# Four products of the filter instead of two sums, added by PE in the transform back, in a stage of attention and hyena

## The chip, the core and the metric

The kernel runs on one core of a Trainium2 chip. The metric is the time of one execution on the device in microseconds (us), lower is better. The engines are PE (TensorE, matmul; its weight loads have a row of their own, PEld), DVE (VectorE), ACT (ScalarE), POOL (GpSimd) and SP (SyncE, which here issues most DMA transfers). Each works through its own queue in order, and they meet only at semaphores. PE writes to PSUM, in banks of 512 fp32 columns.

## What is computed

The reference is a backbone of two layers over 1024 latent tokens and 256 context tokens. Each layer projects its input for three groups of heads (a state space scan, differential attention, and a Hyena convolution of order 2), joins their outputs and projects them back. The change lies in the long convolution:

```python
def _fft_long_conv(u, kf, bias):
    """u (B,L,C), kf (L+1,C) -> two-sided long conv over the whole sequence + bias * u."""
    L = u.shape[1]
    uf = jnp.fft.rfft(u.astype(F32), n=2 * L, axis=1)
    y = jnp.fft.irfft(uf * kf, n=2 * L, axis=1)[:, :L]
    return (y + bias.astype(F32) * u.astype(F32)).astype(u.dtype)

def _hyena(proj, conv_w, conv_b, filt, bias):
    L = proj.shape[1]
    v, x1, x2 = jnp.split(_centred_dwconv(proj, conv_w, conv_b), 3, axis=-1)
    kf = _hyena_kernels_fft(L, filt)
    z = x1 * _fft_long_conv(v, kf[:, 0], bias[0])
    return x2 * _fft_long_conv(z, kf[:, 1], bias[1])
```

`uf * kf` is a product of complex numbers: with X the spectrum of the input and K that of the filter, the real part is Xr Kr - Xi Ki and the imaginary part Xi Kr + Xr Ki.

## The kernel before

Every layer runs stages one after the other, with a barrier between them: normalisation, projections, then `attention_hyena_stage` (L1235), the scan, for the first layer the convolution of the context, and the output projection. `attention_hyena_stage` puts two jobs that have nothing to do with each other into one loop of ticks (`for i in range(NI)`), written once for each engine.

The first job is attention. Its units are (head, tile of 128 queries): 4 x 10 in layer 0 and 4 x 8 in layer 1. In layer 0 the first two tiles of a head are context (I call them short: 256 keys), all others have 1280 keys. A unit passes through several ticks. In tick i PE makes its scores in two halves m = 0 and 1 (L1402, L1403), DVE takes the maximum of each (L1586), ACT the exponential (L1517). A tick later DVE mixes the two halves (L1598). Two ticks later PE turns the mix in up to three batches (L1418), ACT copies each (L1524), and PE multiplies with the values (L1434). After that ACT norms, DVE scales (L1604), PE turns (L1423) and DVE gates (L1611).

The second job is the convolution of 1024 latent tokens, 512 channels in four chunks of 128 and two orders: 8 phases of 4 steps, 32 steps, in ticks 3 to 34. In tick i it is step n = i - 3, and s = n mod 4 is its part of the phase. A step has two of the phase's eight blocks of frequencies:

- PE, `forward` (L1448): 8 matmuls of 128x128 in fp32 (L1460, L1461) from R with the matrices fwd into the PSUM bank pH.
- DVE, `products` (L1613): pH times the spectrum of the filter (K, kn), into R. pt is its scratch tile.
- PE, `backward` (L1464): 8 matmuls (L1475) of R with the matrices inv, into pH again. In order 0 the matrices are the loaded side, in order 1 the data are.
- ACT, `copy_back` (L1539, in the next tick): pH to R (L1542).

Around them DVE has the butterflies: `backs` in the first two ticks of a phase for the phase before, `forth` in the other two for the phase after (`Steps`, L1055 to L1068). In ticks 1 to 13 PE also turns the rows of the convolution's input (`turn_rows`, L1445).

The order within a tick is written out by hand. PE: turn 0, scores 0, forward, turn 1, scores 1, last turn, values, rows, backward. DVE: maximum 0, scale, mix, products, maximum 1, gate, butterflies. ACT: copy back, copy of turn 0, norm, copy of turn 1, exponential 0, last copy, exponential 1. The last 256 columns of scores 1 share a bank with scores 0 and wait for exponential 0. SP loads K two steps ahead into one of two buffers, when the products of the step that used it are done (`y_ready`).

Of the kernel before, what the change touches and what calls it, by code (L numbers as in the profile page):

```python
# [14 lines left out]
ALU = mybir.AluOpType  # L15
# [3 lines left out]
P = 128  # L19
# [141 lines left out]
def sb(nc, ctx, name, shape, dtype=F32):  # L161
    return ctx.enter_context(nc.sbuf_tensor(name, list(shape), dtype))
# [1067 lines left out]
def matrix_block(k, i):  # L1230

    return i if k == 0 else 4 + 3 * (k - 1) + (0, 1, 1, 2)[i]


def attention_hyena_stage(nc, tag, layer, first_tile, ident, lam_vecs, qk_d, v_d, gate_d, hp_d, kf_d, fwd_d, inv_d, o_d):  # L1235
# [29 lines left out]
    with stage(nc, tag + "lam_in", tag + "s00_in", tag + "s01_in", tag + "s10_in", tag + "s11_in", tag + "v0_in", tag + "v1_in",  # L1265
# [1 line left out]
               tag + "turned_copied", tag + "pv_done", tag + "squared", tag + "log_done", tag + "rms_ready", tag + "scaled", tag + "o_turned",  # L1267
               tag + "gated", tag + "stored0", tag + "stored1",
               *(tag + "u%d_in" % c for c in range(4)), *(tag + "x%d_in" % c for c in range(4)), *(tag + "k%d_in" % c for c in range(2)), tag + "kn_in",
               tag + "mats_in", tag + "rows_turned", tag + "rows_copied", tag + "dft_step", tag + "r_ready", tag + "x_mm", tag + "prod_step", tag + "y_ready",  # L1270
               tag + "q_mm", tag + "q_copied", tag + "z_step", tag + "out_ready", tag + "hy_stored") as (ctx, sems):
        (lam_in, s00_in, s01_in, s10_in, s11_in, v0_in, v1_in, lam_step, lam_exp, scored, maxed, exped, mix_step, mixed, turned, turned_copied,
         pv_done, squared, log_done, rms_ready, scaled, o_turned, gated, stored0, stored1) = sems[:25]
        u_in, x_in, k_in = sems[25:29], sems[29:33], sems[33:35]
        (kn_in, mats_in, rows_turned, rows_copied, dft_step, r_ready, x_mm, prod_step, y_ready, q_mm, q_copied, z_step, out_ready, hy_stored) = sems[35:]
        stored = (stored0, stored1)
        score_in = ((s00_in, s01_in), (s10_in, s11_in))
        value_in = (v0_in, v1_in)
# [40 lines left out]
        with nc.Block() as block:  # L1319
            @block.sync  # L1320
            def _(sp):
# [20 lines left out]
                def load_spectra(n):  # L1342
                    p, s = divmod(n, 4)
                    c, o = phases[p]
                    if n >= 2:
                        sp.wait_ge(y_ready, n - 1)
                    sp.dma_start(K[:, n % 2], kf_d[o][:, 4 * s:4 * s + 4, P * c:P * (c + 1)]).then_inc(k_in[n % 2], 16)
                    if s == 0:
                        sp.dma_start(kn[:], kf_d[o][:, 2 * J, P * c:P * (c + 1)]).then_inc(kn_in, 16)
# [6 lines left out]
                for n in range(2):  # L1356
                    load_spectra(n)
# [31 lines left out]
            def _(pe):  # L1389
# [177 lines left out]
            def _(dve):  # L1567
# [45 lines left out]
                def products(n):  # L1613

                    p, s = divmod(n, 4)
                    f = phases[p][0] % 2
                    xs = pH[:].rearrange("p (k a n) -> p k a n", k=2, a=2)
                    kr, ki = (K[:, n % 2, i:4:2].unsqueeze(2).to_broadcast([P, 2, 2, P]) for i in range(2))
                    y = R[:, f, 2 * s:2 * s + 2]
                    dve.wait_ge(k_in[n % 2], 16 * (n // 2 + 1))  # L1620
                    dve.wait_ge(x_mm, n + 1)
                    if n:
                        dve.wait_ge(y_ready, n)
                    if s == 0:
                        dve.wait_ge(kn_in, 16 * (p + 1))
                        dve.tensor_tensor(y[:, 1], xs[:, 1], kr[:, 1], ALU.mult).then_inc(prod_step, 1)
                        dve.tensor_tensor(y[:, 0, 0], xs[:, 0, 0], K[:, n % 2, 0], ALU.mult).then_inc(prod_step, 1)
                        dve.tensor_tensor(y[:, 0, 1], xs[:, 0, 1], kn[:], ALU.mult).then_inc(prod_step, 1)
                    else:
                        dve.tensor_tensor(y, xs, kr, ALU.mult).then_inc(prod_step, 3)  # L1630
                    dve.tensor_tensor(pt[:], xs, ki, ALU.mult).then_inc(prod_step, 1)
                    dve.wait_ge(prod_step, 5 * n + 4)
                    dve.tensor_tensor(y[:, :, 0], y[:, :, 0], pt[:, :, 1], ALU.subtract).then_inc(prod_step, 1)
                    dve.tensor_tensor(y[:, :, 1], y[:, :, 1], pt[:, :, 0], ALU.add).then_inc(y_ready, 1)

                def backs(p, first, last):
                    c, o = phases[p]
# [826 lines left out]
```

## Time and profile before

| | us |
|---|---|
| median of 3 runs | 4172.46 (4168.78 to 4177.13) |
| profiled execution, its own time | 4166.99 |
| its span, first to last instruction | 4164.9 |
| this stage in layer 0, first tick's maximum to the last gate | 1143.6 to 1615.9 |
| this stage in layer 1, first maximum to the last store | 3250.6 to 3683.0 |
| busy in the whole span: PE, PEld, DVE, ACT, POOL | 3522.2, 2889.8, 2521.2, 1081.6, 699.4 |
| mean granted clock of TensorE, share of full speed | 0.928 |

A tick begins where DVE starts its first maximum (L1586, half 0). In layer 1 tick 3 begins at 3284.44, tick 5 at 3307.30, tick 14 at 3421.02 and tick 31 at 3634.49. In layer 0 tick 3 begins at 1174.74, tick 5 at 1197.42, tick 10 at 1260.50, tick 14 at 1307.10, tick 30 at 1502.75 and tick 35 at 1557.07.

### The profile page before, as it was taken

How to read it: one execution, taken by the hardware profiler on the slowest of the kernel's cores; microseconds unless marked ns; L12 is line 12 of the kernel's file. 1: busy time of each engine (PE TensorE's matmuls, PEld its weight loads, DVE VectorE, ACT ScalarE, POOL GpSimd, SP SyncE). 2: the span in 40 equal slices, each digit the busy share in tenths (PEclk: the TensorE clock that was granted, in tenths of full speed). 3: DMA queues.
4: the chain of work that ended last, by engine and by line, in shares of the span. 5: the costliest groups of instructions: out<-in, count | busy, mean ns of one | idle time of the engine just before them, and what ended most of it. 6: DMA issues, size and time to landing. Idle time of an engine off the chain costs nothing. (4 is left out here: it accounts for less than half of the span.)

```text
span 4164.9 us, 51062 instructions
## 1 busy us (share of the span) xinstructions
PE 3522.2 (85%) x19424; PEld 2889.8 (69%) x19424; DVE 2521.2 (61%) x5084; ACT 1081.6 (26%) x1861; POOL 699.4 (17%) x444
## 2 busy tenths in 40 slices
PE   5789999999778875996996788999999688859888
PEld 1677888888667774775782566788888577737577
DVE  3125677754279996765553324667773699967544
ACT  2212222222144443332110311222211344423310
POOL 0132333322100001210000122433343000012000
PEclk8899999999888997998998799999999799989999
DMA  4154223232253312334325145223231633123432
GB/s 174 55 142 144 94 85 97 81 101 74 72 162 97 89 35 74 122 98 150 118 81 187 36 115 163 88 81 97 81 100 62 188 84 84 40 100 105 134 115 71
DMA packets 414110, 424.53 MB, mean 102 GB/s; under 512 B 56908, under 2 KB 350540, under 8 KB 412710
## 3 DMA queue, kind: packets, MB, share of 16 engines
q1 hardware_dynamic: 368844, 319.55, 26.5%
q10 hardware_dynamic: 45024, 101.73, 6.9%
q8 instruction: 155, 2.54, 0.3%
q14 instruction: 87, 0.71, 0.1%
HBM read 288.28 MB, written 124.53 MB: 99 GB/s over the span
## 5 line engine op out<-in xcount | busy, mean ns | idle before, releaser
L665 PE MATMUL l_p_acc<-l_u_hi,l_p_w_hi 128*128 128x512 f32 (+1 forms) x2240 | 612.4, 376 | 49.5 <-POOL l_p_w_lo L580 37.0
L665 PE MATMUL l_p_acc<-l_u_hi,l_p_w_lo 128*128 128x512 f32 (+1 forms) x2240 | 593.5, 367 | 0.0
L665 PE MATMUL l_p_acc<-l_u_lo,l_p_w_hi 128*128 128x512 f32 (+1 forms) x2240 | 592.2, 367 | 0.0
L665 PEld LDWEIGHTS l_p_acc<-l_u_hi,l_p_w_hi 128*128 128x128 f32 x2240 | 390.4, 190 | 127.9 <-POOL l_p_w_lo L580 37.5
L665 PEld LDWEIGHTS l_p_acc<-l_u_hi,l_p_w_lo 128*128 128x128 f32 x2240 | 386.0, 189 | 72.4
L665 PEld LDWEIGHTS l_p_acc<-l_u_lo,l_p_w_hi 128*128 128x128 f32 x2240 | 385.8, 189 | 72.3
L578 POOL TENSOR_TENSOR l_p_w_hi<-l_p_wt,l_p_zero 128x1024 fp32r<-128x1024 f32 x104 | 207.7, 1997 | 983.2 <-PE l_p_acc L665 816.2
L1945 POOL TENSOR_TENSOR l_sd_xend<-l_sd_tok,l_sd_mine 128x512 f32<-128x512 f32 x80 | 85.6, 1072 | 1283.0 <-ACT l_sd_tok L1900 1282.2
L1402 PE MATMUL l_at_pS<-l_at_k_hi,l_at_q 128*128 128x512 f32 (+1 forms) x400 | 167.1, 418 | 147.2 <-ACT l_at_prob L1517 113.9
L580 POOL TENSOR_TENSOR l_p_w_lo<-l_p_wt,l_p_w_hi 128x1024 fp32r<-128x1024 f32 x104 | 271.0, 2606 | 8.2
L1586 DVE TENSOR_REDUCE l_at_nmax<-l_at_pS 128x1 f32<-128x1280 f32 (+1 forms) x144 | 197.1, 1369 | 81.7 <-PE l_at_pS L1403 78.7
L1517 ACT ACTIVATE l_at_prob<-l_at_pS,l_at_nmax 128x1280 f32<-128x1280 f32 (+1 forms) x144 | 177.4, 1232 | 249.5 <-DVE l_at_nmax L1586 249.5
L1402 PEld LDWEIGHTS l_at_pS<-l_at_k_hi,l_at_q 128*128 128x128 f32 x400 | 79.6, 199 | 186.3 <-ACT l_at_prob L1517 142.7
L876 DVE TENSOR_SCALAR l_p_cv<-l_p_stg,l_p_taps 128x1281 f32<-128x1281 f32 (+1 forms) x56 | 85.0, 1517 | 192.6 <-ACT l_p_stg L729 192.2
L822 DVE TENSOR_TENSOR l_p_R<-l_p_sw,l_p_rs 128x512 f32<-128x512 f32 x72 | 49.6, 689 | 228.7 <-PE l_p_sw L644 228.7
L1434 PE MATMUL l_at_pO<-l_at_v,l_at_mixT 128*128 128x128 f32 x1312 | 180.5, 299 | 7.6 <-ACT l_at_mixT L1524 4.5
L1434 PEld LDWEIGHTS l_at_pO<-l_at_v,l_at_mixT 128*128 128x128 f32 x1312 | 174.4, 215 | 10.1 <-issue 6.5
L878 DVE SCALAR_TENSOR_TENSOR l_p_cv<-l_p_stg,l_p_taps,l_p_cv 128x1281 f32<-128x1281 f32 (+1 forms) x56 | 150.8, 2692 | 2.0
L1524 ACT ACTIVATE l_at_mixT<-l_at_pT 128x512 f32<-128x512 f32 (+1 forms) x200 | 104.0, 520 | 181.3 <-PE l_at_pT L1418 181.3
L295 PE MATMUL l_n_pm<-l_n_wa,l_n_cond 128*2 128x512 f32 x192 | 88.0, 616 | 68.5 <-DMA l_n_wa<-w_ada 68.5
L1403 PE MATMUL l_at_pS<-l_at_k_lo,l_at_q 128*128 128x512 f32 (+1 forms) x400 | 144.0, 367 | 0.0
L643 PE MATMUL l_p_sw<-l_p_R,l_p_late 128*128 128x128 f32 x528 | 107.4, 286 | 34.0 <-DVEq L815 34.0
(324 smaller groups left out, 7051.2 us busy)
## 6 DMA issues: line engine op xcount, KB each, us to landing
l_p_wt<-w_in SPq DMA_DIRECT2D x104, 512.0 KB, 3.9
l_n_wa<-w_ada SPq DMA_DIRECT2D x12, 2048.0 KB, 8.2
xbc_d<-l_p_fin ACTq DMA_DIRECT2D x32, 640.0 KB, 2.9
kf_d<-l_p_R SPq DMA_DIRECT2D x72, 256.0 KB, 3.6
l_o_oT<-o_d SPq DMA_DIRECT2D x18, 1024.0 KB, 6.7
l_at_K<-kf_d SPq DMA_DIRECT2D x64, 256.0 KB, 2.9
l_o_rows<-w_out SPq DMA_DIRECT2D x32, 512.0 KB, 4.6
qk_d<-l_p_late ACTq DMA_DIRECT2D x12, 1280.0 KB, 4.8
```

Of the source, the lines that this page charges most:

```text
L295: mm = pe.matmul(pm[0:2, (j % 2) * BANK:(j % 2 + 1) * BANK], cond[:, k], wa[:, j % 2, k], start=(k == 0), stop=(k == KD - 1))
L578: pool.tensor_tensor(w_hi[:, m % 2], wt[:, m % 2], zero[:].unsqueeze(2).to_broadcast([P, KD, P]), ALU.add).then_inc(w_rounded, 1)
L580: pool.tensor_tensor(w_lo[:, m % 2], wt[:, m % 2], w_hi[:, m % 2], ALU.subtract).then_inc(w_split, 1)
L643: pe.matmul(out, mats[:, 4 * k + 2 * e], R[:, k, 0, cols], start=True, stop=False)
L665: mm = pe.matmul(acc[:, a:a + w], (w_hi, w_lo)[wp][:, m % 2, k], (u_hi, u_lo)[up][:, k, t0 + c:t0 + c + w], start=(k == n == 0), stop=(k = ...
L878: dve.scalar_tensor_tensor(cv[:, lo:], stg[:, lo:T + 1], taps[:, 0, tile:tile + 1], cv[:, lo:], ALU.mult, ALU.add).then_inc(conv_step, 1)
L1402: pe.matmul(out, q_s[:, s, m, q * P:(q + 1) * P], k_hi[:, s, m, c:c + w], start=True, stop=False)
L1403: mm = pe.matmul(out, q_s[:, s, m, q * P:(q + 1) * P], k_lo[:, s, m, c:c + w], start=False, stop=True)
L1434: mm = pe.matmul(pO[:, 0:P], mixT[:, kt], v_s[:, h % 2, kt], start=(kt == 0), stop=(kt == keys(q) // P - 1))
L1517: act.activation(prob[:, (2 * n + m) % 3, 0:keys(q)], pS[:, m * T:m * T + keys(q)], ACT.Exp, bias=nmax[:, n % 2, m:m + 1], accum_out=sums[ ...
L1524: act.activation(mixT[:, 4 * b:4 * b + w // P].rearrange("p a b -> p (a b)"), pT[:, 0:w], ACT.Copy).then_inc(turned_copied, 1)
L1586: dve.tensor_reduce(nmax[:, n % 2, m:m + 1], pS[:, m * T:m * T + keys(q)], AX.X, ALU.max, negate=True).then_inc(maxed, 1)
```

## The change

`products` no longer adds. It leaves four real products: Xr Kr and Xi Kr in R as before, and in pt, whose two halves are now ordered by the part that they belong to, -Xi Ki (made with `scalar_tensor_tensor` and the constant -1) and Xr Ki. `backward` multiplies both R and pt with the same inverse matrix and lets PSUM add: 4 matmuls in an accumulation group in place of 2, so 16 in a step in place of 8. The two additions of 256 columns on DVE and its wait for its own products (`prod_step`) go, and so does its wait for the step before. `y_ready` now counts 5 in a step, and PE and SP wait for five times the number.

```diff
@@ load_spectra (SP)
-                        sp.wait_ge(y_ready, n - 1)
+                        sp.wait_ge(y_ready, 5 * (n - 1))
@@ backward (PE)
-                    pe.wait_ge(y_ready, n + 1)
+                    pe.wait_ge(y_ready, 5 * (n + 1))
                     for k in (2 * s, 2 * s + 1):
                         for part in range(2):
                             out = pH[:, (2 * (k % 2) + part) * P:(2 * (k % 2) + part + 1) * P]
                             for i in range(2):
                                 m = inv[:, matrix_block(k, 2 * part + i)]
-                                left, right = (m, R[:, f, k, i]) if o == 0 else (R[:, f, k, i], m)
-                                mm = pe.matmul(out, left, right, start=(i == 0), stop=(i == 1))
+                                for j, product in enumerate((R[:, f, k, i], pt[:, i, k % 2])):
+                                    left, right = (m, product) if o == 0 else (product, m)
+                                    mm = pe.matmul(out, left, right, start=(i == j == 0), stop=(i == j == 1))
@@ products (DVE)
-                    kr, ki = (K[:, n % 2, i:4:2].unsqueeze(2).to_broadcast([P, 2, 2, P]) for i in range(2))
+                    kr, ki = (K[:, n % 2, i:4:2] for i in range(2))
                     y = R[:, f, 2 * s:2 * s + 2]
                     dve.wait_ge(k_in[n % 2], 16 * (n // 2 + 1))
                     dve.wait_ge(x_mm, n + 1)
-                    if n:
-                        dve.wait_ge(y_ready, n)
                     if s == 0:
...
                     else:
-                        dve.tensor_tensor(y, xs, kr, ALU.mult).then_inc(prod_step, 3)
-                    dve.tensor_tensor(pt[:], xs, ki, ALU.mult).then_inc(prod_step, 1)
-                    dve.wait_ge(prod_step, 5 * n + 4)
-                    dve.tensor_tensor(y[:, :, 0], y[:, :, 0], pt[:, :, 1], ALU.subtract).then_inc(prod_step, 1)
-                    dve.tensor_tensor(y[:, :, 1], y[:, :, 1], pt[:, :, 0], ALU.add).then_inc(y_ready, 1)
+                        dve.tensor_tensor(y, xs, kr.unsqueeze(2).to_broadcast([P, 2, 2, P]), ALU.mult).then_inc(y_ready, 3)
+                    dve.tensor_tensor(pt[:, 1], xs[:, :, 0], ki, ALU.mult).then_inc(y_ready, 1)
+                    dve.scalar_tensor_tensor(pt[:, 0], xs[:, :, 1], -1.0, ki, ALU.mult, ALU.mult).then_inc(y_ready, 1)
```

Lines of this stage behind the backward loop stand one higher after the change (the maximum is L1587, the matmul of the transform back L1476).

DVE, the products of one step in layer 1 (part 2 of a phase), with what each instruction waits for. Before:

```order
L1598 SCALAR_TENSOR_TENSOR l_at_mix<-l_at_prob,l_at_back 128x1280 [waits l0_at_turned,l0_at_mix_step]
L1630 TENSOR_TENSOR l_at_R<-l_at_pH,l_at_K 128x512 [waits l0_at_x_mm,l0_at_y_ready,l0_at_k1_in]
L1631 TENSOR_TENSOR l_at_pt<-l_at_pH,l_at_K 128x512
L1633 TENSOR_TENSOR l_at_R<-l_at_R,l_at_pt 128x2x128 [waits l0_at_prod_step]
L1634 TENSOR_TENSOR l_at_R<-l_at_R,l_at_pt 128x2x128
L1586 TENSOR_REDUCE l_at_nmax<-l_at_pS 128x1 [waits l0_at_scored]
```

The same place after:

```order
L1599 SCALAR_TENSOR_TENSOR l_at_mix<-l_at_prob,l_at_back 128x1280 [waits l0_at_turned,l0_at_mix_step]
L1629 TENSOR_TENSOR l_at_R<-l_at_pH,l_at_K 128x512 [waits l0_at_x_mm,l0_at_k1_in]
L1630 TENSOR_TENSOR l_at_pt<-l_at_pH,l_at_K 128x256
L1631 SCALAR_TENSOR_TENSOR l_at_pt<-l_at_pH,l_at_K 128x256
L1587 TENSOR_REDUCE l_at_nmax<-l_at_pS 128x1 [waits l0_at_scored]
```

Between the mix and the second maximum four instructions have become three, and the wait in their middle is gone. (The prefix of a semaphore is printed as that of layer 0 in both layers.)

PE, from the values of a tick over the transform back to the scores of the next, in an order-0 phase of layer 1. Before:

```order
L1434 MATMUL l_at_pO<-l_at_v,l_at_mixT 128x128
L1475 MATMUL l_at_pH<-l_at_inv,l_at_R 128x128 [waits l0_at_y_ready]
L1475 MATMUL l_at_pH<-l_at_inv,l_at_R 128x128 x7
L1418 MATMUL l_at_pT<-ident,l_at_mix 128x128 [waits l0_at_turned_copied,l0_at_gated,l0_at_rows_copied,l0_at_mixed]
L1418 MATMUL l_at_pT<-ident,l_at_mix 128x128 x3
L1402 MATMUL l_at_pS<-l_at_k_hi,l_at_q 128x512 [waits l0_at_exped]
```

The same place after, the end of the 16 matmuls:

```order
L1476 MATMUL l_at_pH<-l_at_inv,l_at_R 128x128
L1476 MATMUL l_at_pH<-l_at_inv,l_at_pt 128x128
L1476 MATMUL l_at_pH<-l_at_inv,l_at_R 128x128
L1476 MATMUL l_at_pH<-l_at_inv,l_at_pt 128x128
L1418 MATMUL l_at_pT<-ident,l_at_mix 128x128 [waits l0_at_turned_copied,l0_at_gated,l0_at_rows_copied,l0_at_mixed]
L1418 MATMUL l_at_pT<-ident,l_at_mix 128x128 x3
L1402 MATMUL l_at_pS<-l_at_k_hi,l_at_q 128x512 [waits l0_at_exped]
```

The matmuls of R and of pt take turns, eight of each, and the next tick's turn and scores stand behind all of them.

## Rows read from the trace of the kernel before

**Rows 1.** Busy time by stretch, layer 1: ticks 3-4, 5-13, 14-30.

```profile
core 0: us, PE busy (x) PEld busy (x) DVE busy (x) ACT busy (x) POOL busy (x), PEclk, DMA share, GB/s
3284.44:3307.30 22.86, 20.44 (x159) 18.91 (x160) 14.47 (x24) 12.29 (x27) 0.00 (x0) 1.00 0.73 214
3307.30:3421.02 113.72, 96.09 (x721) 88.44 (x720) 111.53 (x298) 56.67 (x119) 0.00 (x0) 0.97 0.31 80
3421.02:3634.49 213.47, 172.19 (x1268) 159.36 (x1266) 209.62 (x562) 97.60 (x204) 0.00 (x0) 0.94 0.22 61
```

**Rows 2.** The same view, layer 0: ticks 3-4, 5-9, 10-13, 14-29, 30-34.

```profile
1174.74:1197.42 22.68, 18.88 (x139) 16.76 (x140) 14.46 (x23) 11.49 (x24) 0.00 (x0) 1.00 1.03 279
1197.42:1260.50 63.08, 53.65 (x407) 49.38 (x406) 61.90 (x166) 31.68 (x67) 0.00 (x0) 0.97 0.11 33
1260.50:1307.10 46.60, 36.94 (x245) 33.56 (x245) 43.51 (x133) 19.78 (x48) 0.00 (x0) 0.85 0.26 72
1307.10:1502.75 195.65, 157.67 (x1153) 145.07 (x1151) 192.12 (x533) 86.86 (x189) 0.00 (x0) 0.95 0.34 86
1502.75:1557.07 54.32, 42.09 (x299) 38.09 (x298) 45.58 (x124) 22.85 (x55) 0.00 (x0) 0.94 0.11 37
```

**Rows 3.** The same view, layer 1, four ticks: s0, s1, s2, s3.

```profile
3432.42:3444.65 12.23, 11.17 (x89) 10.47 (x90) 12.05 (x33) 5.74 (x12) 0.00 (x0) 1.00 0.08 23
3444.65:3459.11 14.46, 11.46 (x88) 10.24 (x86) 14.25 (x41) 6.32 (x13) 0.00 (x0) 1.00 0.06 18
3459.11:3471.54 12.43, 9.45 (x61) 9.27 (x62) 12.26 (x34) 5.24 (x11) 0.00 (x0) 0.73 0.20 70
3471.54:3482.94 11.40, 8.72 (x68) 7.83 (x67) 11.08 (x29) 5.62 (x12) 0.00 (x0) 1.00 0.09 25
```

**Rows 4.** Timeline (start, us, engine, line), PE and ACT, s0 tick from 3432.39.

```profile
3432.39 0.49 PE L1460 MATMUL l_at_pH<-l_at_R,l_at_fwd 128*128 128x128 f32 x2 [1.62 <-DVEq L1662]
...
3434.91 0.60 ACT L1524 ACTIVATE l_at_mixT<-l_at_pT 128x512 f32<-128x512 f32 x1 [3.28 <-PE l_at_pT L1418]
...
3435.41 1.32 ACT L1517 ACTIVATE l_at_prob<-l_at_pS,l_at_nmax 128x1280 f32<-128x1280 f32 x1
...
3436.87 0.39 PE L1402 MATMUL l_at_pS<-l_at_k_hi,l_at_q 128*128 128x256 f32 x1 [1.06 <-ACT l_at_prob L1517]
...
3437.55 2.40 PE L1434 MATMUL l_at_pO<-l_at_v,l_at_mixT 128*128 128x128 f32 x20
...
3439.78 1.95 PE L1475 MATMUL l_at_pH<-l_at_inv,l_at_R 128*128 128x128 f32 x16
...
3441.57 0.60 PE L1418 MATMUL l_at_pT<-ident,l_at_mix 128*128 128x128 f32 x4
...
3443.17 0.39 PE L1460 MATMUL l_at_pH<-l_at_R,l_at_fwd 128*128 128x128 f32 x2
```

**Rows 5.** Timeline, PE, tick 13 of layer 1: values, turned rows, transform back.

```profile
3412.56 3.72 PE L1434 MATMUL l_at_pO<-l_at_v,l_at_mixT 128*128 128x128 f32 x20
...
3416.11 0.60 PE L1445 MATMUL l_at_pT<-ident,l_at_hx 128*128 128x128 f32 x4
...
3416.55 1.95 PE L1475 MATMUL l_at_pH<-l_at_inv,l_at_R 128*128 128x128 f32 x16
```

**Rows 6.** Timeline, DVE, tick 14 of layer 1: the products of a step.

```profile
3424.72 0.68 DVE L1630 TENSOR_TENSOR l_at_R<-l_at_pH,l_at_K 128x512 f32<-128x512 f32 x1
...
3425.32 0.68 DVE L1631 TENSOR_TENSOR l_at_pt<-l_at_pH,l_at_K 128x512 f32<-128x512 f32 x1
3426.03 0.43 DVE L1633 TENSOR_TENSOR l_at_R<-l_at_R,l_at_pt 128x256 f32<-128x256 f32 x1
3426.38 0.42 DVE L1634 TENSOR_TENSOR l_at_R<-l_at_R,l_at_pt 128x256 f32<-128x256 f32 x1
3426.71 1.48 DVE L1586 TENSOR_REDUCE l_at_nmax<-l_at_pS 128x1 f32<-128x1280 f32 x1
```

**Rows 7.** Groups by line and form: DVE's form with a constant, 256 columns.

```profile
L1068 DVE SCALAR_TENSOR_TENSOR l_p_R<-l_p_R,l_p_Tm 128x256 f32<-128x256 f32 x64 | 35.8, 600 | 0.4
...
L1068 DVE SCALAR_TENSOR_TENSOR l_p_Tm<-l_p_Tm,l_p_R 128x256 f32<-128x256 f32 x64 | 22.8, 418 | 0.0
```

More of the change, by code:

```diff
@@ L1269, in attention_hyena_stage @@
                *(tag + "u%d_in" % c for c in range(4)), *(tag + "x%d_in" % c for c in range(4)), *(tag + "k%d_in" % c for c in range(2)), tag + "kn_in",
-               tag + "mats_in", tag + "rows_turned", tag + "rows_copied", tag + "dft_step", tag + "r_ready", tag + "x_mm", tag + "prod_step", tag + "y_ready",
+               tag + "mats_in", tag + "rows_turned", tag + "rows_copied", tag + "dft_step", tag + "r_ready", tag + "x_mm", tag + "y_ready",
                tag + "q_mm", tag + "q_copied", tag + "z_step", tag + "out_ready", tag + "hy_stored") as (ctx, sems):
@@ L1274, in attention_hyena_stage @@
         u_in, x_in, k_in = sems[25:29], sems[29:33], sems[33:35]
-        (kn_in, mats_in, rows_turned, rows_copied, dft_step, r_ready, x_mm, prod_step, y_ready, q_mm, q_copied, z_step, out_ready, hy_stored) = sems[35:]
+        (kn_in, mats_in, rows_turned, rows_copied, dft_step, r_ready, x_mm, y_ready, q_mm, q_copied, z_step, out_ready, hy_stored) = sems[35:]
         stored = (stored0, stored1)
@@ L1621, in products @@
                     dve.wait_ge(x_mm, n + 1)
-                    if n:
-                        dve.wait_ge(y_ready, n)
                     if s == 0:
                         dve.wait_ge(kn_in, 16 * (p + 1))
-                        dve.tensor_tensor(y[:, 1], xs[:, 1], kr[:, 1], ALU.mult).then_inc(prod_step, 1)
-                        dve.tensor_tensor(y[:, 0, 0], xs[:, 0, 0], K[:, n % 2, 0], ALU.mult).then_inc(prod_step, 1)
-                        dve.tensor_tensor(y[:, 0, 1], xs[:, 0, 1], kn[:], ALU.mult).then_inc(prod_step, 1)
-                    else:
-                        dve.tensor_tensor(y, xs, kr, ALU.mult).then_inc(prod_step, 3)
-                    dve.tensor_tensor(pt[:], xs, ki, ALU.mult).then_inc(prod_step, 1)
-                    dve.wait_ge(prod_step, 5 * n + 4)
-                    dve.tensor_tensor(y[:, :, 0], y[:, :, 0], pt[:, :, 1], ALU.subtract).then_inc(prod_step, 1)
-                    dve.tensor_tensor(y[:, :, 1], y[:, :, 1], pt[:, :, 0], ALU.add).then_inc(y_ready, 1)
+                        dve.tensor_tensor(y[:, 1], xs[:, 1], kr[:, 1:2].to_broadcast([P, 2, P]), ALU.mult).then_inc(y_ready, 1)
+                        dve.tensor_tensor(y[:, 0, 0], xs[:, 0, 0], K[:, n % 2, 0], ALU.mult).then_inc(y_ready, 1)
+                        dve.tensor_tensor(y[:, 0, 1], xs[:, 0, 1], kn[:], ALU.mult).then_inc(y_ready, 1)
+                    else:
+                        dve.tensor_tensor(y, xs, kr.unsqueeze(2).to_broadcast([P, 2, 2, P]), ALU.mult).then_inc(y_ready, 3)
+                    dve.tensor_tensor(pt[:, 1], xs[:, :, 0], ki, ALU.mult).then_inc(y_ready, 1)
+                    dve.scalar_tensor_tensor(pt[:, 0], xs[:, :, 1], -1.0, ki, ALU.mult, ALU.mult).then_inc(y_ready, 1)
                 def backs(p, first, last):
```

## Prediction

> **What bounds the kernel now.** The change touches one stage, run once per layer: the one that weaves attention with the latent hyena convolution. I read it in this order. First the busy times by stretch [rows 1 to 3]: nearly all of the stage is DVE's. In layer 1, from tick 14 to tick 30, DVE is busy 209.62 of 213.47 us and PE 172.19 [rows 1]. One group of four ticks takes 50.52 us (12.23, 14.46, 12.43 and 11.40), of which DVE works 49.64 and PE 40.80 [rows 3]. I call the four s0, s1, s2, s3 after the part of the transform that they carry. Only ticks 3 and 4 of each layer, where the butterflies of the transform have not yet begun on DVE, are ended by PE: 22.86 and 22.68 us for two, with DVE busy 14.5 of them [rows 1, 2].
>
> A busy share of 81% seems to leave PE room. So second, PE's own loop, from one forward transform to the next [rows 4]. It is a chain over two engines, and its waits do not shrink: the forward transform from 3432.39, behind it the turns, ACT's copy of them at 3434.91, only then (ACT is in order) the exponential at 3435.41, then the last scores, which wait until 3436.87, the values at 3437.55, the transform back at 3439.78, the next turn at 3441.57, scores, and the next forward transform at 3443.17. That is **10.78 us**, and DVE's longest tick hides it with 3.7 us to spare, but its shortest (s3, 11.40) with 0.6. In ticks that also turn rows of the convolution's input, 3 to 13, the loop has 0.44 more (3416.11 to 3416.55) [rows 5].
>
> **What DVE saves.** A step's products start at 3424.72, 3425.32, 3426.03 and 3426.38, and the next maximum at 3426.71: 0.60 + 0.71 + 0.35 + 0.33 = 1.99 us [rows 6]. The 0.71 holds some 0.1 in which DVE waits for its own products. Afterwards there are one product of 512 columns (0.60) and two of 256. An operation of 256 columns takes 0.33 to 0.35 to the next start, with both ends in SBUF; from PSUM it can't be above the 0.60 of the 512-column product, which reads PSUM. The second one has the form with a constant, which no row shows on PSUM; in SBUF that form has a mean of 418 ns at best and 600 ns at worst for 256 columns, against 426 ns for the plain subtraction [rows 6, 7]. I take 0.34 for both, since the best row equals the plain one and the worst comes from another stage: 1.28 us, **a saving of 0.71 us** per step. With the worst row it is 0.53. The s0 steps split the first product in three in both kernels and save the same. Nothing can hide a saving on an engine that is 98% busy, so it counts wherever DVE ends the tick.
>
> **What PE pays.** The transform back has 8 products more, 16 instructions more in the trace, where each of these fp32 matmuls is two. The 16 of before take from 3439.78 to 3441.57 [rows 4]: 1.79 us, 112 ns each. The added ones have the same shape, half of them from the tile pt and not from R, so I take 1.79 again. The lower bound is half of it, 0.9 us, if two matmuls in a row with the same inverse matrix loaded (the case in the order-0 steps) were cheaper; the upper is what half clock makes of it, 3.6. There are 64 steps (32 in each layer), so PE gets 115 us of work and DVE loses 45 us. The new work stands in PE's in-order queue ahead of the next turn and scores, so nothing can be put over it: **the loop is 10.78 + 1.79 = 12.57 us, 13.01 with rows to turn.**
>
> The Trainium skill, page "TensorE: Matmul & The Clock Gate", section "Back-to-back issue gap", gives about 81 ns per matmul of 128 columns in a stream of loads and matmuls. By that figure the added work is an estimated 1.30 us, the loop 12.08, and the time about 4175 us, no change. The trace has 112 ns, and I go by it.
>
> **The edits that cost nothing.** The removed wait of DVE on its own earlier step and the semaphore with other counts cost nothing, since their events lie a tick back. The reload of the filter's tile waits for the same step as before. pt is now read by PE; DVE overwrites it in the next step, after the next forward transform, which stands behind the transform back in PE's queue, so that adds no wait either.
>
> **Tick by tick.** DVE's ticks become 11.52, 13.75, 11.72 and 10.69 us: 47.7 for four. PE's loop makes 50.3 of them. A long s1 of DVE delays the next maximum by 1.3 us but not PE, because the exponential waits for ACT's copy until 3.0 us behind the forward transform anyway. So a group takes about 50.4 us, as much as now: the gain of DVE is used up and PE sets the pace.
>
> Layer 1. Ticks 3 and 4: 22.86 to 26.0, +3.2. Ticks 5 to 13: 113.72 to 9 x 13.01 = 117.1, +3.4. Ticks 14 to 30: 213.47 to 17 x 12.57 = 213.7, and some 0.1 for each s1, +0.6 [rows 1]. The last four steps stand alone in a chain (forward, products, back, copy) with no attention of other tiles to fill it: 4 x (1.79 - 0.71) = +4.3. Sum **+11.5**.
>
> Layer 0 has ten tiles per head and not eight; two are short text tiles, around which PE has less to do. Ticks 3 and 4: 22.68 to 26.0, +3.3. Ticks 5 to 9: 63.08 to 3 x 13.01 + 13.75 + 11.72 = 64.5, +1.4. Ticks 10 to 13 (46.60): the first two are now ended by PE, +1.2 and +1.4; in the third DVE stays later, -0.7; the fourth is ended by PE at half clock already (the clock is 0.85 over the four), +1.8: +3.7. Ticks 14 to 29 (195.65): five long s3 and s0 ticks get +3.8 together (12.57 for 11.40 or 12.23), one short one +0.4, one -0.4, and in nine DVE ends the tick as before, 9 x -0.71: -2.5. Ticks 30 to 34 (54.32): -0.1, +0.9, -0.7, and twice +1.8 where DVE has no butterflies left to do (it is busy 45.58): +3.7. Sum **+9.6** [rows 2].
>
> Together +21.1 us. The profiled execution took 4166.99 (span 4164.9), so 4188.1; the median of the runs is 5.5 higher, and so is my number: 4172.5 + 21.1 = **4193.6**.
>
> **Rivals.**
> First, **DVE keeps the bound** and PE's work is hidden (faster). Then 54 steps give 0.71 each, -38 us, and only the ten that PE ended before or that stand alone cost some +17: -21 us, 4151. This needs 1.08 us of room in PE's loop in every tick. For it: DVE at 98%, PE at 81% [rows 3]. Against: in s3 the loop has 0.6, and its idle time is the wait for an exponential, which new matmuls behind it cannot fill. It decides from a loop below 10.7 us after the change. Half the price for the added matmuls (0.9) would go most of this way: loop 11.67, DVE ends s0, s1 and s2, some -6.5 per layer, 4159. The Trainium skill, page "Perfetto Trace Analysis", section "Identifying the Most-Contended Engine", says to find the engine of highest occupancy and optimize it first; by that rule this rival holds, and the trace agrees on DVE's occupancy but shows the loop beside it. Chance 0.13 for both together.
>
> Second, **the halved clock moves into the loop** (slower by more). In each group PE now idles ahead of s2 and then runs at the lower of its two levels, 1.2 and not 2.4 GHz: the granted clock is 0.73 of full speed over that tick, and 1.00 over the other three [rows 3]. A tile's values then take 3.72 us and not 2.40 [rows 4, 5]. DVE hides that today. If it stayed, the loop would pay 1.3 for the values and about 1.5 for the transform back, 2.8 us in each of some 11 groups: +31, 4224. Against: with the added work PE's long idle stretch shrinks to the 1.06 us that it waits for the exponential in other ticks [rows 4], behind which the clock is full. Chance 0.12.
>
> Third, **no change that can be measured**: a loop of about 12.1 us, because something in it overlaps that I count in a row (scores of the next tile behind the transform back, say), 4172 to 4180. Chance 0.13.
>
> **How the numbers follow.** My forecast, PE's loop at 12.57 us and full clock, has 0.62. 0.2% (8.3 us) is about what a measurement of this kernel can tell from no change. Faster: 0.13. Same: 0.13 and a little of the forecast's lower edge, 0.15. Slower: 0.72. The range: 4166 leaves out the first rival (0.13), and 4222 the upper half of the second (0.06). The worst price of the form with a constant moves only the ticks that DVE ends, some 20 of them, by 0.18 each: +4, inside.
>
> **What would show it.** In the profile after: (1) the form with a constant at 0.42 us, products to next maximum 1.28 us; (2) 16 more instructions in each transform back, 3.6 us in all; (3) forward to forward 12.57 us in s3 and s0, DVE's maximum now waiting for PE's scores there (it hardly waits now), with DVE's busy share near 93% and PE's near 91%; (4) ticks 3 and 4 together 26 us; (5) a granted clock of 1.00 in s2. A group of four ticks well below 50 us would prove the prediction wrong on the loop; one of 53 or more with a clock below 0.9, on the clock.

## Result: slower by 0.4%, with PE's loop in DVE's place

The changed kernel takes 4186.86 us in the median of 8 runs (4179.89 to 4189.81), the kernel before 4170.91 us on the same chip (4162.93 to 4177.13, 8 runs). The ratio is 1.0038, 95% interval 1.0027 to 1.0049: **slower by 0.38%, 16 us**. The forecast was 21 us slower. (Here and below a difference in us follows the ratio, which uses all runs; the times given are medians.)

The profiled execution of after took 4189.75 us (span 4187.7 against 4164.9). Its page first: the busy times of the engines, and the group of DVE's maximum, after and before, in the layout "busy, mean ns | idle before, releaser".

```profile
PE 3607.7 (86%) x20448; PEld 2980.8 (71%) x20448; DVE 2480.4 (59%) x5020; ACT 1081.0 (26%) x1861; POOL 698.8 (17%) x444
...
L1587 DVE TENSOR_REDUCE l_at_nmax<-l_at_pS 128x1 f32<-128x1280 f32 (+1 forms) x144 | 197.0, 1368 | 133.9 <-PE l_at_pS L1403 132.9
...
L1586 DVE TENSOR_REDUCE l_at_nmax<-l_at_pS 128x1 f32<-128x1280 f32 (+1 forms) x144 | 197.1, 1369 | 81.7 <-PE l_at_pS L1403 78.7
```

Both halves of the change are there. DVE works 40.8 us less (2521.2 before) in 64 instructions fewer. PE has 1024 instructions more, 16 in each of 64 steps, and works 85.5 us more. By the durations behind it those 1024 instructions are 64 x 1.79 = 115 us; that the busy time grew by less has one cause in work that runs at a higher clock than before, as the next rows show (the value matmuls, L1434, are busy 163.8 us and were 180.5). DVE's idle time ahead of the maximum, nearly all of it the wait for PE's scores, was 81.7 us and is 133.9 now.

Where the time went, by the same stretches as [rows 1, 2]. Layer 1, ticks 3-4, 5-13, 14-30:

```profile
core 0: us, PE busy (x) PEld busy (x) DVE busy (x) ACT busy (x) POOL busy (x), PEclk, DMA share, GB/s
3298.20:3324.21 26.01, 23.81 (x191) 22.45 (x192) 13.06 (x21) 12.30 (x27) 0.00 (x0) 1.00 0.66 192
3324.21:3441.46 117.25, 106.90 (x858) 100.29 (x857) 105.23 (x290) 56.02 (x118) 0.00 (x0) 1.00 0.30 78
3441.46:3653.69 212.23, 193.53 (x1549) 181.66 (x1548) 197.74 (x545) 97.76 (x205) 0.00 (x0) 1.00 0.23 61
```

Layer 0, ticks 3-4, 5-9, 10-13, 14-29, 30-34:

```profile
1178.04:1201.62 23.58, 21.89 (x171) 20.65 (x172) 13.06 (x21) 11.48 (x24) 0.00 (x0) 0.98 0.99 268
1201.62:1265.80 64.18, 58.46 (x472) 54.78 (x470) 58.41 (x160) 30.26 (x63) 0.00 (x0) 1.00 0.11 32
1265.80:1315.25 49.45, 42.95 (x323) 39.97 (x324) 40.62 (x130) 20.69 (x52) 0.00 (x0) 0.93 0.27 74
1315.25:1508.67 193.42, 176.31 (x1400) 165.11 (x1399) 181.04 (x516) 86.94 (x190) 0.00 (x0) 0.99 0.33 86
1508.67:1566.64 57.97, 51.26 (x388) 47.84 (x387) 42.09 (x118) 22.88 (x56) 0.00 (x0) 0.94 0.10 35
```

Against before that is, in layer 1, +3.15, +3.53 and -1.24 us, and in layer 0 +0.90, +1.10, +2.85, -2.23 and +3.65. With +3.6 in the last steps of layer 1 and -0.6 in its ticks 0 to 2, the two stages account for some +15 us of the +22.8 between the two profiled executions. The rest lies in stages whose instructions are the same in both kernels, and nothing shows that it is the change's. Up to the first maximum of layer 0 the traces of the ten kernels profiled here, all with the same instructions, take from 1141.6 to 1148.4 us (before 1143.6, after 1146.8). From tick 35 of layer 0 to the first maximum of layer 1, where they have the same instructions too (four of them in another order in the first four ticks), they take from 1682.8 to 1698.3 us, and after's is the longest (before's 1693.5).

One group of four ticks of layer 1 (s0, s1, s2, s3), the counterpart of [rows 3]:

```profile
3453.84:3466.37 12.53, 11.46 (x94) 10.76 (x93) 11.36 (x32) 5.80 (x13) 0.00 (x0) 1.00 0.08 22
3466.37:3480.09 13.72, 12.65 (x105) 11.96 (x104) 13.54 (x40) 6.11 (x14) 0.00 (x0) 1.00 0.07 20
3480.09:3491.78 11.69, 10.47 (x85) 9.77 (x84) 11.55 (x32) 5.78 (x12) 0.00 (x0) 1.00 0.22 75
3491.78:3503.81 12.03, 10.96 (x89) 10.27 (x89) 10.38 (x28) 5.33 (x12) 0.00 (x0) 1.00 0.07 22
```

49.97 us, where it was 50.52. s1 and s2, where DVE is busy to within 0.2 us of the tick, gained 0.74 each. s0 and s3 lost 0.30 and 0.63: DVE idles 1.2 and 1.65 us in them. And the granted clock of s2 is 1.00 now, where it was 0.73.

PE's loop in this group, from one forward transform to the next (timeline: start, us, engine, line, with the idle time ahead in brackets), the counterpart of [rows 4]:

```profile
3466.10 0.38 PE L1460 MATMUL l_at_pH<-l_at_R,l_at_fwd 128*128 128x128 f32 x2
...
3470.48 0.39 PE L1402 MATMUL l_at_pS<-l_at_k_hi,l_at_q 128*128 128x256 f32 x1 [1.06 <-ACT l_at_prob L1518]
...
3471.15 2.40 PE L1434 MATMUL l_at_pO<-l_at_v,l_at_mixT 128*128 128x128 f32 x20
3473.38 0.39 PE L1476 MATMUL l_at_pH<-l_at_inv,l_at_R 128*128 128x128 f32 x2
3473.61 0.39 PE L1476 MATMUL l_at_pH<-l_at_inv,l_at_pt 128*128 128x128 f32 x2
...
3476.96 0.60 PE L1418 MATMUL l_at_pT<-ident,l_at_mix 128*128 128x128 f32 x4
...
3478.55 0.38 PE L1460 MATMUL l_at_pH<-l_at_R,l_at_fwd 128*128 128x128 f32 x2
```

12.45 us. The forward transforms of this group and the next start at 3453.64, 3466.10, 3478.55, 3491.16 and 3503.61, so the four loops take 12.46, 12.45, 12.61 and 12.45 us. That is 49.97 together, the length of the group: although DVE fills s1 and s2, PE's loop sets the total. The wait for the exponential is still there, 1.06 us as before, and the transform back takes 3.58 us (3473.38 to 3476.96), twice 1.79. On DVE, the products of this tick:

```profile
3470.06 0.68 DVE L1629 TENSOR_TENSOR l_at_R<-l_at_pH,l_at_K 128x512 f32<-128x512 f32 x1
3470.66 0.41 DVE L1630 TENSOR_TENSOR l_at_pt<-l_at_pH,l_at_K 128x256 f32<-128x256 f32 x1
3471.00 0.41 DVE L1631 SCALAR_TENSOR_TENSOR l_at_pt<-l_at_pH,l_at_K 128x256 f32<-128x256 f32 x1
3471.33 1.48 DVE L1587 TENSOR_REDUCE l_at_nmax<-l_at_pS 128x1 f32<-128x1280 f32 x1
```

1.27 us from the first product to the maximum.

### The profile page after: what moved, and what is told of

Read it like the earlier page. It is cut to its first block and busy times, and to the rows that moved or that the text cites. A ratio compares the mean times of both kernels' runs of the same rounds, so it can differ in the third digit from the quotient of the medians.

```text
span 4187.7 us, 52984 instructions
## 1 busy us (share of the span) xinstructions
PE 3607.7 (86%) x20448; PEld 2980.8 (71%) x20448; DVE 2480.4 (59%) x5020; ACT 1081.0 (26%) x1861; POOL 698.8 (17%) x444
## 5 line engine op out<-in xcount | busy, mean ns | idle before, releaser
L1942 POOL TENSOR_TENSOR l_sd_xend<-l_sd_tok,l_sd_mine 128x512 f32<-128x512 f32 x80 | 85.5, 1071 | 1298.6 <-ACT l_sd_tok L1897 1297.7
L1587 DVE TENSOR_REDUCE l_at_nmax<-l_at_pS 128x1 f32<-128x1280 f32 (+1 forms) x144 | 197.0, 1368 | 133.9 <-PE l_at_pS L1403 132.9
L1434 PE MATMUL l_at_pO<-l_at_v,l_at_mixT 128*128 128x128 f32 x1312 | 163.8, 281 | 4.5 <-ACT l_at_mixT L1525 4.5
L1434 PEld LDWEIGHTS l_at_pO<-l_at_v,l_at_mixT 128*128 128x128 f32 x1312 | 157.1, 197 | 6.5 <-issue 6.5
```

The source lines that it names most:

```text
L1434: mm = pe.matmul(pO[:, 0:P], mixT[:, kt], v_s[:, h % 2, kt], start=(kt == 0), stop=(kt == keys(q) // P - 1))
L1587: dve.tensor_reduce(nmax[:, n % 2, m:m + 1], pS[:, m * T:m * T + keys(q)], AX.X, ALU.max, negate=True).then_inc(maxed, 1)
```

## Experiments

The theory: a tick ends with the later of two chains, DVE's queue and PE's loop. The change shortens the first by 0.71 us and lengthens the second by 1.79, and each counts only where its chain is the later one. The rivals: DVE hides PE's work, and the loss has another cause (the reads of pt, the new form on DVE); or the prices simply add, whatever the tick.

**Each half of the change alone.** First DVE's saving without PE's price:

```diff
-                                for j, product in enumerate((R[:, f, k, i], pt[:, i, k % 2])):
-                                    left, right = (m, product) if o == 0 else (product, m)
-                                    mm = pe.matmul(out, left, right, start=(i == j == 0), stop=(i == j == 1))
+                                left, right = (m, R[:, f, k, i]) if o == 0 else (R[:, f, k, i], m)
+                                mm = pe.matmul(out, left, right, start=(i == 0), stop=(i == 1))
```

> The changed kernel, but the transform back multiplies only the tile R, 8 matmuls as before the change. It leaves out the two products with the filter's imaginary part from what is transformed back; they are still computed on DVE. So it has DVE's saving without PE's price. Theory (PE's loop at 10.78 us is short enough for DVE to set the pace again, and each step saves 0.71 us where DVE ends the tick): 54 steps x 0.71 = -38 us against the kernel before, ratio 0.991; a group of four ticks of layer 1 takes 50.52 - 2.84 = 47.7 us, products to next maximum 1.27 us. Rival (DVE's saving is partly hidden by PE's loop already at the old price): s3 would stay at its 11.40 us and less than -30 us would show, ratio 0.993 or above.

Then PE's price without DVE's saving, on the kernel before:

```diff
-                            for i in range(2):
+                            for i in (0, 1, 0, 1):
```

> The kernel before, but every accumulation of the transform back is made twice (the second time with start set again, so the output is the same): 8 matmuls more per step, DVE as before. So it has PE's price without DVE's saving. Theory (two chains, the later one ends the tick; loop 12.57 us against DVE's ticks of 12.23, 14.46, 12.43, 11.40): only ticks shorter than the loop grow, s0 12.5, s1 14.4, s2 12.5, s3 12.5 at most, a group 51.2 to 51.9 us and not 50.52; layer 1 +18 us, layer 0 +15 us, together about +33 us, ratio 1.008. Rival (DVE hides PE's matmuls, and what the change costs comes from something else, such as the reads of pt by PE or the new form on DVE): +10 us or less, ratio below 1.003. Additive prices (no coupling): the result of this run and of the one with half the transform back would sum to the change's own +16 us; by the theory they sum to about -5.

Measured: the first 4124.7 us, ratio 0.9888 (0.9874 to 0.9901), -47 us. The second 4209.96 us, ratio 1.0093 (1.0079 to 1.0107), +39 us. The same four ticks by stretch, first of the kernel with DVE's saving alone:

```profile
3404.14:3415.64 11.50, 10.43 (x82) 9.73 (x83) 11.35 (x32) 5.88 (x13) 0.00 (x0) 1.00 0.09 24
3415.64:3429.35 13.71, 12.16 (x94) 10.94 (x92) 13.54 (x40) 6.34 (x13) 0.00 (x0) 1.00 0.07 19
3429.35:3441.04 11.69, 8.70 (x60) 8.53 (x61) 11.55 (x33) 5.25 (x11) 0.00 (x0) 0.85 0.22 75
3441.04:3451.70 10.66, 8.89 (x70) 8.01 (x68) 10.37 (x29) 5.73 (x12) 0.00 (x0) 1.00 0.09 26
```

and of the kernel with PE's price alone:

```profile
3462.08:3474.60 12.52, 11.45 (x94) 10.76 (x93) 12.05 (x32) 5.80 (x13) 0.00 (x0) 1.00 0.08 23
3474.60:3489.05 14.45, 13.38 (x112) 12.69 (x111) 14.24 (x40) 6.13 (x14) 0.00 (x0) 1.00 0.07 19
3489.05:3501.48 12.43, 10.49 (x86) 9.80 (x84) 12.26 (x33) 5.84 (x12) 0.00 (x0) 1.00 0.20 70
3501.48:3512.88 11.40, 10.24 (x82) 9.35 (x80) 11.08 (x30) 5.36 (x11) 0.00 (x0) 1.00 0.08 24
```

With the old transform back all four ticks shrink, by 0.73 to 0.75, and DVE is busy to within 0.3 us of each: 47.56 us. With 16 matmuls and the old DVE work the group grows only from 50.52 to 50.80 us, less than the 51.2 expected, and the growth sits in s0 alone, since the others are still DVE's. (In the next two groups s0 is 12.79.) Its 39 us come mostly from elsewhere: +12.3 and +12.5 us in ticks 3 to 13 of layers 0 and 1, and +4.9 in the lone steps at the end of layer 1. So the reads of pt and the new form on DVE aren't needed for the loss: the matmuls make it. And the prices don't add: -47 and +39 are -8 together, the change itself is +16. The 24 us between (17.6 in the traces, where the two stages whole changed by -43.8, +41.0 and +14.8 us) are saving that DVE can't turn into time once PE's loop is there. The first run was 9 us better than forecast. In its trace the two stages have 41.6 us less up to tick 30 (tick 33 in layer 0). The -38 had left out tick 4, which gained 0.4 us in each layer, and tick 3 and tick 13 of layer 0, 11.16 to 10.42 and 14.22 to 11.89 us. Of the last 5 us, 2.3 are in the last steps of layer 1; the others are in neither stage.

**Is each us of loop a us of tick?** The changed kernel with 24 matmuls in each transform back:

```diff
+                            for i in range(2):
+                                m = inv[:, matrix_block(k, 2 * part + i)]
+                                left, right = (m, R[:, f, k, i]) if o == 0 else (R[:, f, k, i], m)
+                                pe.matmul(out, left, right, start=(i == 0), stop=(i == 1))
```

(These lines stand ahead of the loop over R and pt.)

> The changed kernel with a third set of 8 matmuls in each transform back (the products of R are accumulated once more ahead and then overwritten by the restart, so the output is the same): 24 matmuls, DVE as in the changed kernel. Theory (PE's loop ends every tick but s1, which is 13.72 us by DVE): loop 12.57 + 1.79 = 14.36 us, now above DVE's longest tick too; each of the four ticks 14.4 us, a group 57.4 us against 49.97, so 1 us of loop costs 1 us of tick; over some 54 steps and the tail about +110 us against the changed kernel, ratio against the kernel before 1.03. Rival (half of the added time is covered, since PE stood idle before the exponential and DVE is also near its limit): below +60 us, ratio below 1.018.

Measured: 4287.33 us, ratio 1.0277 (1.0263 to 1.0291), +100 us against the changed kernel. The four ticks:

```profile
3518.34:3532.64 14.30, 13.23 (x110) 12.54 (x109) 11.36 (x31) 5.80 (x13) 0.00 (x0) 1.00 0.07 19
3532.64:3546.81 14.17, 13.10 (x109) 12.41 (x108) 13.63 (x40) 5.67 (x13) 0.00 (x0) 1.00 0.07 20
3546.81:3561.11 14.30, 13.23 (x110) 12.54 (x109) 11.56 (x31) 5.80 (x13) 0.00 (x0) 1.00 0.18 61
3561.11:3575.27 14.16, 13.09 (x109) 12.40 (x108) 10.38 (x28) 5.66 (x13) 0.00 (x0) 1.00 0.06 19
```

All four ticks are alike now, though DVE's work in them runs from 10.38 to 13.63 us: 56.93 us, or 14.23 a tick. That is the loop bare, and it is 1.78 us above 12.45. PE is busy 13.1 to 13.2 us in each of these ticks: **an engine that sets every tick alone, with 1.07 us of idle in each.** Its share is 92.5%, and all of the missing part is the wait for the exponential. The +100 is 10 short of the forecast: the loop is 14.23 and not 14.36, and some ticks of layer 0 are still DVE's (tick 32 takes 12.66 us where it took 12.65).

**Is that wait part of the loop?** Nothing in the values needs this exponential. So four of their ten products (key tiles 0 to 3) go ahead of the last 256 columns of scores:

```diff
                     for c, w in pieces:
                         out = pS[:, m * T + c:m * T + c + w]
+                        if ahead is not None and w == CTX:
+                            values(ahead, 0, 4)
                         if w == CTX and q >= CT and n + m:
                             pe.wait_ge(exped, 2 * n + m)
```

The rest of the values follows where it was. The same edit was made in both kernels; in the kernel before it is the control.

> The changed kernel with another order on PE: the first four value matmuls of a long tile (key tiles 0 to 3, whose weights have long been turned and copied) are issued ahead of the last 256-column piece of scores, that is, into the 1.06 us in which PE waits for ACT's exponential. Same work, same instructions. Theory (PE's loop sets the pace, and this idle 1.06 us is part of it): loop from 12.57 to about 11.6 us, a group of four ticks of layer 1 from 49.97 to about 48.6 us, the kernel about -24 us against the changed one, ratio against the kernel before about 0.998. Rival (something else than the loop keeps the ticks at 12.5 us, DVE or the DMA of the filter): no change from the changed kernel, ratio 1.004.

> The kernel before with the same other order on PE: four value matmuls ahead of the last piece of scores. The control. Theory (DVE ends nearly all ticks, so PE's idle 1.06 us costs nothing): only ticks that PE ends gain, -4 to -6 us, ratio 0.9988; the group of four ticks of layer 1 stays at 50.5 us. Rival (the order is better by itself, on any kernel): as much as in the changed kernel, -20 us or more, ratio 0.995.

Measured: in the changed kernel 4158.46 us, ratio to before 0.9971 (0.9962 to 0.9981), -28 us against the changed kernel (21 of them in the two stages by the traces). In the kernel before 4169.15 us, ratio 0.9997 (0.9988 to 1.0006): nothing, where -4 to -6 was expected. Its small gains, such as 0.85 us in tick 33 of layer 0, were lost again elsewhere: ticks 9 and 13 of layer 1 grew from 12.43 to 13.21. The four ticks in the changed kernel:

```profile
3431.68:3443.31 11.63, 11.46 (x94) 10.91 (x93) 11.35 (x32) 5.80 (x13) 0.00 (x0) 1.00 0.08 23
3443.31:3457.02 13.71, 13.54 (x112) 12.99 (x111) 13.54 (x39) 6.12 (x14) 0.00 (x0) 1.00 0.07 20
3457.02:3468.72 11.70, 10.74 (x84) 9.77 (x83) 11.56 (x33) 5.85 (x12) 0.00 (x0) 1.00 0.22 75
3468.72:3479.38 10.66, 10.55 (x82) 9.49 (x80) 10.37 (x29) 5.37 (x11) 0.00 (x0) 1.00 0.08 25
```

s0 is 0.90 shorter and has PE busy 11.46 of 11.63 us. s3 is down to 10.66, which is DVE's own time: its saving counts there at last (11.40 in the kernel before). The group is 47.70 us. Same instructions, another order: the wait was part of the loop, and the change left it there. In ticks 4 to 7, 10 and 11 of layer 1, which turn rows too, the edit brought only 0.2 to 0.3 a tick (12.58 against 12.83 in s3). The trace shows what holds the loop there (tick 6 of layer 1, DVE's gate and PE's turned rows, L1612 and L1445 in the changed kernel):

```profile
3323.19 0.28 DVE L1616 TENSOR_TENSOR l_at_g<-l_at_pT,l_at_g 128x128 f32<-128x128 f32 x1
...
3323.57 0.63 PE L1448 MATMUL l_at_pT<-ident,l_at_hu 128*128 128x128 f32 x4 [0.45 <-issue]
```

`turn_rows` waits for `gated`, and the gate stands behind the products and the second maximum in DVE's queue. PE idles 0.45 us and starts 0.10 us after the gate's end; so it does in ticks 4 to 12 of this kernel wherever it waits there, and in the kernel with PE's price alone. In these ticks the two chains aren't apart: a part of DVE's work lies inside PE's loop. That is why the kernel with PE's price alone needs 13.31 to 13.50 us in ticks 4 to 7 of layer 1, and the changed kernel, with DVE's saving, 12.83 to 12.96.

**The same change, only where DVE ends the tick.**

```diff
+        def apart(n):
+            i = n + FIRST_STEP
+            return i in ((8, 9, 12, 16, 17, 20, 21, 22, 23, 24, 25, 28, 29, 32) if first_tile == 0 else (8, 9, 12, 13, 16, 17, 20, 21, 24, 25, 28, 29))
```

Where it is false, `products` adds on DVE as before, and `backward` takes R alone.

> The new form of a step (products apart, 16 matmuls back) only in ticks that DVE ended in the kernel before (layer 0: 8, 9, 12, 16, 17, 20 to 25, 28, 29, 32; layer 1: 8, 9, 12, 13, 16, 17, 20, 21, 24, 25, 28, 29), the old form in all others; same output. Theory (a tick is the later of DVE's chain and PE's loop, so the same edit gains 0.71 us where DVE is later and costs where PE is): a group of four ticks of layer 1 about 12.23 + 13.72 + 11.70 + 11.40 = 49.05 us, and not 50.52 or 49.97; 26 steps x -0.71, with about +1 each at the four that turn rows in their tick and are s2, together -16 us, ratio 0.996. Rival (the new form costs by its number of steps, whatever the tick): about 26/64 of the change's +16, +6 us, ratio 1.0015.

Measured: 4155.56 us, ratio 0.9961 (0.9948 to 0.9973), -16 us and faster, with the same edit that is slower when it is made everywhere. The rival, a price per step at +6, falls. But that the -16 was hit is luck. In the trace the two stages whole have only 6.1 us less than before, and the other 10 are in neither. Some ticks didn't come as expected. The s2 ticks 17 and 21 of layer 1, and then PE's timeline in each:

```profile
3446.76:3459.73 12.97, 10.64 (x73) 9.99 (x72) 11.56 (x33) 5.23 (x11) 0.00 (x0) 0.87 0.19 67
...
3497.23:3508.93 11.70, 9.37 (x76) 8.73 (x75) 11.56 (x33) 5.55 (x12) 0.00 (x0) 1.00 0.72 207
```

```profile
3449.75 0.39 PE L1407 MATMUL l_at_pS<-l_at_k_hi,l_at_q 128*128 128x256 f32 x1 [2.33 <-ACT l_at_prob L1523]
...
3450.43 4.03 PE L1439 MATMUL l_at_pO<-l_at_v,l_at_mixT 128*128 128x128 f32 x20
```

```profile
3500.22 0.39 PE L1407 MATMUL l_at_pS<-l_at_k_hi,l_at_q 128*128 128x256 f32 x1 [2.33 <-ACT l_at_prob L1523]
...
3500.89 2.40 PE L1439 MATMUL l_at_pO<-l_at_v,l_at_mixT 128*128 128x128 f32 x20
```

In both PE waits 2.33 us for the exponential. In tick 17 the values then take 4.03 us, with a granted clock of 0.87 over the tick, and in tick 21 they take 2.40 at 1.00. So the second rival of the prediction, the lower clock level inside the loop, does exist: here, in ticks 17, 25 and 29, at 1.27 us each, and in tick 25 of layer 0 (12.96 us at 0.87). Tick 10 of layer 0 takes 10.38 us and tick 30 too, where they took 9.27 and 9.26. What decides between tick 17 and tick 21, after equal waits, stays open.

**The best places.** The new form in ticks 8, 12, 14 to 30 (and 32 in layer 0), the old one elsewhere, and the early values from tick 14 on; then the same with the new form in ticks 9 and 13 as well. The first of the two, as edits of the two kernels above:

```diff
-            return i in ((8, 9, 12, 16, 17, 20, 21, 22, 23, 24, 25, 28, 29, 32) if first_tile == 0 else (8, 9, 12, 13, 16, 17, 20, 21, 24, 25, 28, 29))
+            return i in ((8, 12, *range(14, 31), 32) if first_tile == 0 else (8, 12, *range(14, 31)))
...
-                    early = turning == 3 and i < NU and units[i][1] >= CT
+                    early = i >= 14 and turning == 3 and i < NU and units[i][1] >= CT
```

> The new form in ticks 8, 12, 14 to 30 (and 32 in layer 0), the old form elsewhere, and four value matmuls ahead of the last piece of scores from tick 14 on. Theory, summed tick by tick from the traces of the kernel before and of the changed kernel with that order: layer 1 ticks 14 to 30 213.5 to 203.1 us, -10.4; layer 0 the same ticks -10.4; ticks 8, 12, 32 -0.7 each, -3.6; together -24.5 us, ratio 0.994, faster than the kernel before and than every other with the same output. Rival (the gains of neighbouring ticks take each other's place: PE's lead gained in old-form ticks is what DVE-ended ticks live on): half of it, -12 us, ratio 0.997.

> As the kernel with the new form at 8, 12, 14 to 30 and the early value matmuls, but with the new form at ticks 9 and 13 of both layers as well, where DVE ended the tick before by 12.43 us and the loop with rows to turn is 10.78 + 0.44 = 11.22 us in the old form and 13.01 in the new. Theory: these s2 ticks go to 12.6 us (as in the changed kernel's own trace), +0.2 each and not -0.71, and layer 0's tick 13 from 14.2 to 14.9: +1 us in all, no difference that can be measured from its neighbour, ratio 0.994. Rival (DVE's 0.71 us counts there, because DVE ended these ticks): -2.8 us.

Measured: 4140.43 us, ratio 0.9927 (0.9913 to 0.994), and 4138.46 us, ratio 0.9921 (0.9908 to 0.9935). Both are faster than either kernel, by some 30 to 33 us against before, and not to be told apart from each other. By the traces the two stages have 23.1 and 22.7 us less than before in their ticks (to tick 30, and to tick 33 in layer 0), which is close to the 24.5 that was expected; the rest isn't in them, and I can't place it. Ticks 9 and 13 with the new form are 12.64 us in layer 1, as the theory says. In layer 0 tick 9 gains 0.79 by it (11.71 for 12.50) and tick 10 loses 1.05.

## Why the prediction was right, and where it was not

**DVE's saving** was put at 0.71 us, 1.99 to 1.28. It is 1.99 to 1.27, 0.72. The open point was the form with a constant on PSUM: 0.41 us for 256 columns, the same as the plain product ahead of it, and start to start 0.33. The best row of [rows 7] was the right bound. The 600 ns row was not: it is a mean, and the median of its 64 instructions is 419 ns, the longest 2611.

**PE's price** was put at 1.79 us with 0.9 and 3.6 as its bounds. The transform back takes 3.58, so it is 1.79. Those rows are of an order-1 step, where the data are loaded. In an order-0 step, where two matmuls in a row have the same inverse matrix loaded, it is the same, 3.57 us (tick 6 of layer 1, its beginning and the next turn):

```profile
3344.63 0.39 PE L1476 MATMUL l_at_pH<-l_at_R,l_at_inv 128*128 128x128 f32 x2
3344.85 0.39 PE L1476 MATMUL l_at_pH<-l_at_pt,l_at_inv 128*128 128x128 f32 x2
...
3348.20 0.60 PE L1418 MATMUL l_at_pT<-ident,l_at_mix 128*128 128x128 f32 x4
```

A repeated loaded side saved nothing. (A row names the loaded side last, as in `l_at_k_hi,l_at_q` for `pe.matmul(out, q_s, k_hi)`. By that, the two lists of PE's order in "The change" and [rows 4], with `l_at_inv,l_at_R`, are of order-1 phases; the text calls the lists order 0.) The Trainium skill ("TensorE: Matmul & The Clock Gate", section "Back-to-back issue gap") would have given 81 ns and, as an estimate, a loop of 12.08; the trace has 112 ns in this kernel too, and the measurement decides.

**The loop** was the step on which all rested, and it held: a second chain beside an engine that was 98% busy, which ends the tick once it has grown by 1.79. Its size was off by 0.12: 12.57 was forecast, 12.45 measured. The loop read in [rows 4] began with a forward transform that had waited, 4.48 us to the last scores and not 4.38 as when it runs through. With rows to turn it is 12.83 to 12.96 us and not 13.01. Seventeen ticks of 0.12 are 2 us in layer 1, which is the miss there: -1.24 in place of +0.6. The group is 49.97 us where 50.4 was forecast.

**Tick by tick.** Layer 1's ticks 3-4 (+3.15, forecast +3.2) and 5-13 (+3.53, +3.4) and the lone steps at its end (+3.6, +4.3) came as worked out. In layer 0, ticks 5-9 (+1.10, +1.4), 14-29 (-2.23, -2.5) and 30-34 (+3.65, +3.7) did as well; 10-13 gave +2.85 for +3.7, with the miss in tick 13 (+0.71 for +1.8). (The +3.8 in ticks 14-29 was added up wrongly: three times 1.17 and twice 0.34 are 4.2.) The term that failed is layer 0's ticks 3 and 4: +0.90 for +3.3. I gave tick 3 the loop's 13 us because layer 1's has it. But in layer 0 that tick was never a whole loop, 11.16 us before and 10.69 after. The tile whose values it multiplies is a short one, and before the change PE waited in it 0.55 us for the products, ahead of the transform back, and 1.33 us behind it, ahead of the next turn. In the changed kernel the transform back starts at once, and the added matmuls fill that second wait. With 2.4 us there, 1.8 in layer 1's ticks 14-30, and smaller misses, the sum of 21 comes down to the +15 of the traces and the +16 of the timing.

**The first rival**, DVE keeps the bound, was refuted where it was to decide: it needed a loop below 10.7 us. The rule it came from (the Trainium skill, "Perfetto Trace Analysis", section "Identifying the Most-Contended Engine") names DVE here, and to relieve DVE was worth 47 us, as the first experiment shows; what it doesn't weigh is the engine that gets the work. **The second**, the halved clock, was argued away for this kernel rightly in all but one tick: 1.00 in s2 where it was 0.73. PE's wait for the exponential in that tick went from 4.82 to 1.22 us. The two halves of the change show which one did it: with PE's price alone the same tick has a wait of 1.94 us and a clock of 1.00, with DVE's saving alone 3.48 us and 0.85. The exception is tick 25 of layer 0, 12.94 us at 0.87 where ticks 17 and 29 take 11.69 at 1.00; there PE waited 1.96 us and the values took 3.46:

```profile
1448.38 0.58 PE L1402 MATMUL l_at_pS<-l_at_k_hi,l_at_q 128*128 128x256 f32 x1 [1.96 <-ACT l_at_prob L1518]
...
1449.61 3.46 PE L1434 MATMUL l_at_pO<-l_at_v,l_at_mixT 128*128 128x128 f32 x20
```

In the mixed kernel, with the old form in s0 and s3, PE idled 2.33 us in s2 and the lower clock came back in more ticks. **The third**, a loop of 12.1, fell with 12.45.

**The signs named** were: the form with a constant at 0.42 us (0.41), 3.6 us of transform back (3.58), 12.57 forward to forward (12.45), DVE near 93% and PE near 91% (93.2% and 91.2% over ticks 14 to 30), ticks 3 and 4 together 26 us (26.01 in layer 1, not in layer 0), a clock of 1.00 in s2.

## What to carry to other kernels

A busy share says which engine to relieve, not which may be given the work. Before moving work, follow the receiving engine around its own loop, waits on others included, and compare that with the tick: here PE at 81% had 0.6 us of room in its tightest tick, and was given 1.79. The receiving engine's loop can also run through the relieved engine, as it does here in the ticks that turn rows; then the two prices can't be told apart by tick. When the loop had become the bound, the cheapest next step here was not to undo the change but to put independent work into the wait inside the loop (28 us, worth nothing before the change), and to make the change only in those ticks that the relieved engine ends.

## What was not expected of the hardware

After an equal wait of 2.33 us the same 20 matmuls once took 4.03 us at a tick's granted clock of 0.87 and once 2.40 at 1.00. And PE's added work cost less of its busy time than it took: 115 us of matmuls raised the busy time by 85.5, since, for one, ticks 14 to 30 of layer 1 went from a granted clock of 0.94 [rows 1] to 1.00 once PE idled less. The slow stretches of the kernel before hardly reached its end, since DVE covered them (s2 of [rows 3] is 12.43 us at 0.73, with DVE busy 12.26); those of the mixed kernel did, at 1.27 us each.
